# Recurrence heads of a two-layer transformer kernel: one head at a time through logarithms, or two at a time through products of gates

## The reference, cut to what matters

```python
def _hgrn2_direction(q, f_logit, v, lb):
    f = lb + (1.0 - lb) * sigmoid(f_logit)
    return _gla_chunkwise(q, 1.0 - f, v, log(f))
# S_t = diag(f_t) S_{t-1} + k_t v_t^T ;  o_t = S_t^T q_t     with k = 1 - f
o_fwd = _hgrn2_direction(q, ff, v, lb_fwd)
o_bwd = flip(_hgrn2_direction(flip(q), flip(fb), flip(v), lb_bwd))
o = rmsnorm(o_fwd + o_bwd, norm_g) * silu(hg)
```

## Time and profile before

| | |
|---|---|
| time, median of 3 runs | 2187.49 us (2187.25 to 2187.61) |
| profiled execution, span from first to last instruction | 2186.0 us |
| TensorE, matmuls | 2164.6 us busy, 99% |
| TensorE, weight loads | 1817.7 us, 83% |
| VectorE / ScalarE | 1452.0 us, 66% / 1031.1 us, 47% |
| HBM | 227 GB/s over the span |
| granted TensorE clock | 0.999 of full speed |

### The profile page before, as it was taken

The page is one execution under the profiler, slowest core; times in us unless marked ns, Lnnn a source line. Parts: engine busy times, 40 slices in busy tenths (PEclk is TensorE's granted clock), DMA queues, the critical chain, the costliest instruction groups (busy, mean ns, idle before and its releaser), DMA issues.

```text
span 2186.0 us, 25174 instructions
## 1 busy us (share of the span) xinstructions
PE 2164.6 (99%) x10675; PEld 1817.7 (83%) x10675; DVE 1452.0 (66%) x1415; ACT 1031.1 (47%) x1034; POOL 5.5 (0%) x17
## 2 busy tenths in 40 slices
PE   8999999999999999999999999999999999999998
PEld 8878888877888788778889988888888888888886
DVE  5778667775775777877866676484646645654756
ACT  5443573343435743443464556575434433443442
POOL 0000000000000000000000000000000000000000
PEclk9999999999999999999999999999999999999999
DMA  8867648584996548649853325374756656655753
GB/s 287 313 237 289 235 170 346 216 305 155 371 337 240 209 186 334 247 185 344 315 201 109 121 102 184 116 263 162 267 194 226 221 194 209 248 192 193 269 189 119
DMA packets 73071, 497.28 MB, mean 227 GB/s; under 512 B 9040, under 2 KB 9472, under 8 KB 16384
## 3 DMA queue, kind: packets, MB, share of 16 engines
q1 hardware_dynamic: 72640, 495.59, 62.2%
q10 hardware_dynamic: 320, 0.09, 0.0%
HBM read 491.42 MB, written 4.23 MB: 227 GB/s over the span
## 4 chain that ended last, share of the span: by engine, by line
PE 95%; DVE 3%; DMA 1%; ACT 1%; issue 0%; DVEq 0%; SPq 0%; ACTq 0%
PE products L2525 51%; PE products L2536 14%; PE aside L2525 6%; PE products L3260 4%; PE aside L3260 4%; PE products L3262 2%; PE aside L3262 2%; PE aside L2691 1%; PE aside L2845 1%; PE aside L2964 1%; DMA raw<-in_w_a_idx 1%; DMA raw<-in_w_mlp 1%; DVE w_low L1555 1%; PE products L2907 0%; PE aside L2659 0%; ACT w_high L885 0%
## 5 line engine op out<-in xcount | busy, mean ns | idle before, releaser
L1555 DVE TENSOR_TENSOR w_low<-raw,w_high 128x2048 fp32r<-128x2048 f32 (+3 forms) x319 | 704.3, 2211 | 501.0 <-ACT w_high L885 500.3
L885 ACT ACTIVATE w_high<-raw 128x2048 fp32r<-128x2048 f32 (+3 forms) x319 | 590.0, 1852 | 776.2 <-PE products L2525 412.4
L2525 PE MATMUL products<-w_high,x_high_and_low 128*128 128x512 f32 (+2 forms) x2496 | 756.0, 381 | 10.1 <-DVE w_low L1555 9.1
L2525 PEld LDWEIGHTS products<-w_high,x_high_and_low 128*128 128x128 f32 x2496 | 462.3, 189 | 97.0 <-issue 11.4
L2525 PE MATMUL products<-w_low,x_high_and_low 128*128 128x512 f32 (+2 forms) x1248 | 472.2, 378 | 0.0
L2525 PEld LDWEIGHTS products<-w_low,x_high_and_low 128*128 128x128 f32 x1248 | 235.5, 189 | 42.5 <-issue 1.7
L2536 PE MATMUL products<-w_high,x_high_and_low 128*128 128x512 f32 (+1 forms) x784 | 260.4, 393 | 0.0
L1569 DVE SCALAR_TENSOR_TENSOR raw<-raw,cond_row 128x2048 f32<-128x2048 f32 x96 | 219.2, 2284 | 0.0
L2536 PEld LDWEIGHTS products<-w_high,x_high_and_low 128*128 128x128 f32 x784 | 147.4, 188 | 25.9 <-issue 0.6
L2536 PE MATMUL products<-w_low,x_high_and_low 128*128 128x512 f32 (+1 forms) x392 | 150.4, 384 | 0.0
L2525 PE MATMUL products<-w_high,u_high 128*128 128x512 f32 x304 | 118.4, 390 | 0.0
(11 more groups left out here) (416 smaller groups left out, 2549.2 us busy)
## 6 DMA issues: line engine op xcount, KB each, us to landing
raw<-in_w_mlp SPq DMA_DIRECT2D x128, 1024.0 KB, 4.9
raw<-in_w_mod SPq DMA_DIRECT2D x96, 1024.0 KB, 5.1
raw<-in_w_ple SPq DMA_DIRECT2D x32, 1024.0 KB, 6.7
raw<-in_w_a_qkv SPq DMA_DIRECT2D x24, 1024.0 KB, 6.2
raw<-in_w_b_kvq SPq DMA_DIRECT2D x24, 1024.0 KB, 7.4
raw<-in_w_a_gate SPq DMA_DIRECT2D x16, 1024.0 KB, 6.1
raw<-in_w_a_out SPq DMA_DIRECT2D x16, 1024.0 KB, 7.1
raw<-in_w_b_gate SPq DMA_DIRECT2D x16, 1024.0 KB, 6.0
```

The lines of the kernel that those rows point to most:

```text
L885: act.activation(split_tile(m, 0, st, u, j, 0, n), m.raw[:, RAW_SLOT[at], 0:n], ACT.Copy).then_inc(m.s_w_high, 1)
L1555: dve.tensor_tensor(lo, m.raw[:, RAW_SLOT[at], 0:n], hi.bitcast(F32), ALU.subtract).then_inc(m.s_raw_used, 1)
L2525: ins = pe.matmul(bank, x[:, x0 + kk, a], w, start=first and kk == 0 and n == 0, stop=last and kk == st.kq - 1 and n == 2)
```

## The change

Two heads are now one batch, four batches of 12 steps, and a step is one of the 48 slots. Logarithms, the table of spans, its DMAs and its rounding, the span matmuls and the exponentials are gone. In their place the gates themselves are transposed (they were before too, but only to make k = 1 - f) and kept. VectorE keeps for both heads four strips of 512 (`m.h_w`: two kinds of keys, two kinds of queries) and doubles their spans level by level, starting with neighbours: the right halves of one pair of strips times the product of the left span's gates, the left halves of the other times the right span's, and then the spans' own products for the next level (`spans_doubled`). Before each doubling ScalarE lays out from these strips the level's keys and queries, two copies of 512 (`m.h_op`, two buffers in turn). TensorE multiplies them a step later, four matmuls into one of the two banks of `m.t`, and VectorE takes the level's pairs under its mask a step after that. TensorE may not write a bank of `m.t` for level i before VectorE has taken level i - 2 out of it (`s_h_red`). The last batch ends in slot 47; nothing of the heads is left in `uq`.

The core of the diff, ScalarE's part first, then VectorE's, then TensorE's:

```diff
+def crossed(x, left, right, half):
+
+
+    d = kind(x, left)
+    return bass.AP(tensor=d.tensor, offset=d.offset, ap=[d.ap[0], [2 * half, BH * T // (2 * half)], [BH * T * (right - left) + half, 2], [1, half]])
...
+def span_products(m, i):
+
+
+    return m.h_f[:] if i == 0 else m.h_p[:, 1024 - (2048 >> i):1024 - (1024 >> i)]
...
+        b, step = divmod(n, STEPS)
+        if step == 0:
...
+            forget = m.g[:, 2:4].rearrange("p h (d t) -> p d h t", d=2)
+            act.activation(m.h_qt[:], m.u[:, 0], ACT.Copy).then_inc(m.s_h_qc, 1)
+            act.activation(m.h_f[:].rearrange("p (d h t) -> p d h t", d=2, h=BH), forget, ACT.Copy).then_inc(m.s_h_fc, 1)
+            keys = m.h_w[:].rearrange("p (d h t) -> p d h t", d=4, h=BH)[:, 0:4:3]
+            act.activation(keys, forget, ACT.Identity, scale=-1.0, bias=1.0).then_inc(m.s_h_k1, 1)
+        if step == 3:
...
+        i = step - 2
+        if 0 <= i < LEVELS - 1:
+            half, k = 1 << i, (LEVELS - 1) * b + i
+            act.wait_ge(m.s_h_mul, LEVELS * b + i + 1)
+            if i == 0:
+                act.wait_ge(m.s_h_k1, b + 1)
+            if k >= 2:
+                act.wait_ge(m.s_h_am, products_before(k - 2) + 1)
+            for n, (left, right) in enumerate(((0, 3), (1, 2))):
+                operand = kind(m.h_op[:, k % 2], n).rearrange("p (s a e) -> p s a e", a=2, e=half)
+                act.activation(operand, crossed(m.h_w, left, right, half), ACT.Copy).then_inc(m.s_h_op, 1)
...
+    def chosen(b, i):
+
+
+        own = m.h_at[:, b % 2, 0].rearrange("p h b t -> p (h b) t")
+        mask = m.h_mask[:, LEVELS - 2 - i:LEVELS - 1 - i, :].broadcast_to((P, BH * RB, P))
+        dve.wait_ge(m.s_h_red, (LEVELS - 1) * b + i)
+        dve.copy_predicated(own, mask, m.t[:, i % 2].rearrange("p (a t) -> p a t", t=P)).then_inc(m.s_h_red, 1)
...
+    def spans_doubled(i):
+
+
+        half = 1 << i
+        totals = span_products(m, i).rearrange("p (s a) -> p s a", a=2)
+
+        def by(side):
+            return totals[:, :, side:side + 1].broadcast_to((P, totals.shape[1], half))
+
+        suffixes, prefixes = (m.h_w[:, 2 * BH * T * n:2 * BH * T * (n + 1)].rearrange("p (s a e) -> p s a e", a=2, e=half) for n in range(2))
+        lane.sync()
+        lane.did(dve.tensor_tensor(prefixes[:, :, 1, :], prefixes[:, :, 1, :], by(0), ALU.mult))
+        dve.tensor_tensor(suffixes[:, :, 0, :], suffixes[:, :, 0, :], by(1), ALU.mult).then_inc(m.s_h_mul, 1)
+        if i < LEVELS - 2:
+            lane.did(dve.tensor_tensor(span_products(m, i + 1), totals[:, :, 0], totals[:, :, 1], ALU.mult))
 
...
     def heads_slot(n):
...
-        if h < HH and s == 3:
-            dve.wait_ge(m.s_h_qc, h + 1)
-            decayed(h, 0)
-        if h < HH and s == 5:
-            decayed(h, 1)
-            if h + 1 < HH:
-                log_f_low(h + 1)
+        b, step = divmod(n, STEPS)
+        if step == 1:
+            dve.wait_ge(m.s_h_qc, b + 1)
+            dve.wait_ge(m.s_h_fc, b + 1)
+            back, forward = kind(m.h_w, 1), kind(m.h_w, 2)
+            lane.did(dve.tensor_tensor(forward, m.h_qt[:], m.h_f[:, 0:BH * T], ALU.mult))
+            dve.tensor_tensor(back, m.h_qt[:], m.h_f[:, BH * T:2 * BH * T], ALU.mult).then_inc(m.s_h_mul, 1)
+            dve.wait_ge(m.s_h_k1, b + 1)
+            dve.tensor_tensor(m.h_ks[:], kind(m.h_w, 0), kind(m.h_w, 3), ALU.add).then_inc(m.s_h_kc, 1)
+        i = step - 2
+        if 0 <= i < LEVELS - 1:
+            dve.wait_ge(m.s_h_op, 2 * (LEVELS - 1) * b + 2 * i + 2)
+            if i == 0:
+                dve.wait_ge(m.s_h_kc, b + 1)
+            spans_doubled(i)
+        i = step - 4
+        if 0 <= i < LEVELS - 1:
+            dve.wait_ge(m.s_h_am, LEVELS * b + i + 1)
+            if i == 0:
+                dve.wait_ge(m.s_h_a0, b + 1)
+            chosen(b, i)
...
-    def spans(h, group, dr, banks):
-
-        md = m.h_md[:, dr]
-        for blk in range(RB):
-            bank = banks[:, blk]
-            for first, lf in ((True, m.h_lfh[:, dr, blk]), (False, m.h_lfl[:, dr, blk])):
-                if group:
-                    ins = pe.matmul(bank, lf, md[:, 5:9, :].rearrange("p l t -> p (l t)"), start=first, stop=not first)
...
-        ins.then_inc(m.s_h_d, 1)
...
+        i = step - 3
+        if 0 <= i < LEVELS:
+            k = (LEVELS - 1) * b + i
+            if i < LEVELS - 1:
+                pe.wait_ge(m.s_h_op, 2 * k + 2)
+            else:
+                pe.wait_ge(m.s_h_mul, LEVELS * b + LEVELS)
...
+            if i >= 2:
+                pe.wait_ge(m.s_h_red, k - 1)
+            for hh in range(BH):
+                for blk in range(RB):
+                    own, other = T * hh + P * blk, T * hh + P * (1 - blk)
+                    if i < LEVELS - 1:
+                        keys, queries = m.h_op[:, k % 2, own:own + P], m.h_op[:, k % 2, BH * T + own:BH * T + own + P]
+                    else:
+                        keys, queries = kind(m.h_w, 3 * blk)[:, own:own + P], kind(m.h_w, 2 - blk)[:, other:other + P]
+                    ins = pe.matmul(m.t[:, i % 2, own:own + P], keys, queries, start=True, stop=True)
             ins.then_inc(m.s_h_am, 1)
...
-            if st is uq and j == 0:
-                heads_slot(6 * HH + 2)
...
             if st is uq and j == 2:
-                heads_slot(6 * HH + 5)
```

More of the change, by code:

```diff
@@ L43 @@
 LEVELS = 8
+BH, STEPS = 2, 12
+BATCHES = HH // BH
 WORDS = 24704
@@ L808, in unit_by_unit @@
                     bring(m.h_l0[:, dr, slot, :], rows(lb[slot], 1024), m.s_h_rows)
[L809 to L812, removed]
     for name in ("c_f", "c_hq", "c_hi", "c_mla", "c_hg", "uq", "ukv"):
@@ L1208, in scalar_program @@
     high_unit("c_hq", 0, [3])
-    def log_f(u):
-        act.wait_ge(m.s_h_fr, u + 1)
-        act.activation(m.h_lf[:, :, 512 * u:512 * u + 512], m.pf[:, :, 512 * u:512 * u + 512], ACT.Ln).then_inc(m.s_h_logf, 1)
[L1214 to L1218, removed]
-        else:
-            log_f(3)
-    gemm("c_hq", queries, late=2)
-    def log_f_high(h):
-        if h:
-            act.wait_ge(m.s_h_d, 4 * h)
-        else:
-            act.wait_ge(m.s_h_logf, 4)
-        lf = m.h_lf[:].rearrange("p r (a c) -> p a r c", a=2)[:, :, :, HD * h:HD * h + HD]
-        act.activation(m.h_lfh[:], lf, ACT.Copy).then_inc(m.s_h_lfh, 1)
@@ L2224, in vector_program @@
     ukv = PLAN["ukv"]
[L2225 to L2226 removed]
+    h_mean_squares(slice(0, HH - BH), HH - BH)
+    h_mean_squares(slice(HH - BH, HH), HH)
+    h_inverse_std(slice(0, HH - BH), 1)
     for rb in range(RB):
@@ L3301, in shape_constants @@
     rates = np.tile(np.concatenate([inverse(500000.0, ROT_A), inverse(500000.0, ROT_I), inverse(10000.0, ROT_M)]), (P, 1))
-    tau, spans = s, np.zeros((P, 2, 9, P))
-    def span(mid, right):
-        fwd = np.where(right, (mid <= tau) & (tau <= t), (t < tau) & (tau < mid))
-        bwd = np.where(right, (mid <= tau) & (tau < t), (t <= tau) & (tau < mid))
-        return fwd, bwd
-    def level(l):
-        half = P >> l
-        return span(t // (2 * half) * (2 * half) + half, t % (2 * half) >= half)
-    order = [span(P, np.zeros((1, P), bool))] + [level(l) for l in range(1, 4)]
-    order += [span(0, np.ones((1, P), bool))] + [level(l) for l in range(4, LEVELS)]
-    for n, pair in enumerate(order):
-        for dr in range(2):
-            spans[:, dr, n] = pair[dr]
     masks = [(s // (P >> l) // 2 == t // (P >> l) // 2) & (s // (P >> l) != t // (P >> l)) for l in range(1, LEVELS)]
     masks = np.ascontiguousarray(np.stack(masks, axis=1).reshape(P, -1), dtype=np.uint8)
-    out = {"consts": const, "rates": rates, "spans": spans.reshape(P, -1)}
+    out = {"consts": const, "rates": rates}
     return {"level_masks": masks, **{k: np.ascontiguousarray(v, dtype=np.float32) for k, v in out.items()}}
@@ L3398, in program @@
     d.rates = a["rates"]
-    d.spans = a["spans"]
     d.level_masks = a["level_masks"]
```

288 lines of the change are left out of this document (86 added, 202 removed).

## The result

The changed kernel takes 2160.65 us (median of 4 runs, 2160.51 to 2162.70) where the kernel before took 2187.51 beside it (2187.25 to 2187.61): 26.9 us less, a ratio of 0.988 (95% interval 0.9868 to 0.9892). The forecast was 2161.5, and its range 2155 to 2169. The profiled execution's span is 2158.7 us, 27.3 less than 2186.0. The 0.4 between the two gains comes from comparing executions: wherever both are on record, the time lies 1.9 to 2.0 us above the span in the changed kernel and 1.8 to 1.9 in the kernel before, so the span of 2186.0 belongs to an execution of some 2187.8, and the 1.5 given with it in front is too small.

The account below looks back on a forecast made before the run. TensorE's full list in the heads' stage was taken as the bound: 32.5 us shed less 6.5 of waits gives 26.0, so the median falls from 2187.5 to 2161.5 us; range 2155 to 2169.

Parts of the forecast that it names:

- What bounds the stage: Heads' stage: TensorE, busy 201.67 of 201.98 us, sets the time, so whatever leaves its list leaves the time.
- The spans' 31.0: TensorE in the heads: removing the span matmuls, 3.88 us for each of 8 heads, saves 31.0 us.
- The rest of the shed: TensorE beyond the spans: 1.5 us from dense operands, 0.9 from a vanished wait, less 0.9 for added returns.
- The strided operands: TensorE's level products: dense copies replace queries read in short runs, saving 0.19 us per head, 1.5 in all.
- the 0.9 priced for the added returns: TensorE: more returns from plain f32 to rounded weights, 44 instead of some 33 at 0.085 us, cost 0.9 us.
- The waits' 6.5: TensorE's level slots: nine waits for VectorE's choosing, 5.1 us, plus 1.4 of restarts, cost 6.5 us.
- the slot-by-slot walk: All 48 slots, each instruction starting when engine and semaphores allow: 5.1 us of waits, 2.2 in batch 3.
- ScalarE's copies: ScalarE's level copies: pace 0.51 us, level 0 perhaps 0.77 for single elements; no cost taken, up to 1.5 us allowed.
- No waits at all: Rival for the level slots: the chain has cover enough, only TensorE's list counts, 2155.0 us; chance 0.10.
- A chain that paces most slots: Rival for the level slots: dearer chain instructions give waits of 9 to 14 us, 2164 to 2169; chance 0.20.
- Rival 3: Level slots: chain at 1.8 times the price, waits pass 32.5 us, slower than before; 2197 at twice; chance 0.03.
- A return of the time in `uq`: Rival in `uq` or the MLA: ScalarE or VectorE holds TensorE later, 1 to 3 us; full return has chance 0.02.

Follow-up runs that it names:

- half the spans: The kernel before with the h_log_f_low matmuls left out of every call of spans, half of the span matmuls; 2173.69 us.
- the run with 1.2 us a level: The changed kernel with two more 512-wide VectorE products ahead of the doubling in six of a batch's seven levels; 2181.84 us.
- the choosing ahead: The changed kernel with VectorE's choosing of level i-2 placed ahead of the doubling for level i; 2154.11 us.
- both edits of the order: The changed kernel with VectorE's choosing ahead of its doubling and the rotation of the MLA's shared key moved from slot 40 to 46; 2153.53 us.
- dense copies: The changed kernel with ScalarE's copies of levels 0 and 1 reading one dense strip instead of elements in turn from two; 2160.62 us.

## Why the prediction was right, step by step

**What bounds the stage.** Held. The list of TensorE was the time before (half the spans: 15.6 off the list, 14.7 off the stage; 13.5 off the time), and it still is: 171.94 of 176.87 us.

**The spans' 31.0.** Held by the same run: half of them is 15.5 by my rows and 15.6 by its busy time.

**The rest of the shed.** The sum was 32.5. Measured it is 35.0: stage and `uq` are 28.0 shorter, in spite of slots 7.0 us longer than undisturbed ones. The term mis-sized is that of the plain f32 matmuls and their turns. The strided operands cost 2.0, not 1.5. And I priced a group of level products at 8 times 0.107 and 0.085 for the return, from a run of 16; the rows after:

```profile
1123.20 1.05 PE L2949 MATMUL aside<-h_operands 128*128 128x128 f32 x8
1124.01 0.48 PE L2493 MATMUL products<-w_high,x_high_and_low 128*128 128x512 f32 x1
1124.32 0.40 PE L2493 MATMUL products<-w_low,x_high_and_low 128*128 128x512 f32 x1
```

The group takes 0.81, not 0.86, which is 32 times 0.045 or 1.4 us. Its eight starts are 0.11 apart (1.05 less the last record's 0.27, over seven), and the rounded matmul behind it starts only some 0.03 after the last. So short groups are cheaper than a share of a long one, and this more than offsets the 0.9 priced for the added returns. The remaining 0.6 us of the 2.5 I don't split.

**The waits' 6.5.** Measured 7.0: 4.8 in seven brackets (5.1 in nine forecast; by batch 0.5, 1.2, 0.7 and 2.4 for 0.7, 1.1, 1.1 and 2.2) and 0.2 a wait around them where I took 0.15, with small delays in slots that show no bracket. The place and size of the largest, 2.10 in slot 42 for 2.2, came out of the slot-by-slot walk, and so did its cause: without the rotation it is 0.27. The mechanism (level i - 2 chosen one doubling too late) is shown three ways: by another order, by a third bank, and by longer work on VectorE.

**ScalarE's copies.** Level 0 has a pace of 0.75 where I expected "perhaps 0.77", level 1 0.61 where I expected 0.51. The prediction's nearest row was read a little too clean: the seventh of VectorE's eight products lasts 0.48, not 0.42, and the strips are 513 and 1537 elements apart, not 1024 or more. The Trainium skill (SBUF — State Buffer, section "Door 1: The DMA port swizzle") puts the limit at two accesses in a 16-byte line, by which runs of two would be free; on ScalarE they paid 0.10 a copy, and only runs of four were free. I held the whole at 0 to 1.5 us; it is at most 0.5.

**The rivals.** No waits at all (2155.0) failed, and is what one bank more makes true. A chain that paces most slots failed: seven of 28 level slots wait. The run with one product more shows how near it was: 0.6 us on VectorE a level, and the gain falls from 26.9 to 17.1. Rival 3's price was 0.48 on six instructions a pair of slots, some 1.4 us a level, from where it would pass 2187; the run with 1.2 us a level stands at 2181.84, so the point was about right. A return of the time in `uq` failed (27.25 us, 2.9 less, as forecast); but 1.0 us does come back later, 0.7 of it at the wait for `mix` (the offset between the two traces is 28.1 us ahead of that wait and 27.4 behind it).

**Why the median was met.** 35.0 less 7.0, and 0.2 for the earlier start, less 1.0 that came back, is 27.2, the span's 27.3. I had 26.0 by a shed 2.5 too small, waits 0.5 too small, and nothing for `mix`: the errors cancel in part.

**What stays open.** The wait for `mix` is 0.5 us here, 0.5 with half the spans, 0.3 with three banks, none with the choosing ahead, and 0.5 again with both edits of the order. In each kernel with a shorter heads' stage ScalarE has a wait of 1.0 to 1.8 us there for a transfer of `in_w_mlp`, 0.8 and 0.4 in the two with the long one. The kernel with one product more has that wait (1.0) and none for `mix`. Why the transfer comes later relative to the work wasn't tried, and neither was whether it causes TensorE's wait. Open too is what the lower clock costs in a stage that has other waits (above).

## What to carry to other kernels

When a chain over two engines feeds a full TensorE, walk its slots with measured prices and ask at each PSUM bank who must read it before the next write; what stands between that read and its data in the reader's queue is the wait. Issue the read that frees a bank ahead of work that waits for something else, or give the bank a third partner: 6 to 7 us here, for no work more. Average idle time (VectorE's third) says nothing of this. And a walk is only as good as the place of each instruction in its queue: two products on the wrong side of a wait made a forecast of 6.6 us where 10.6 came.

## What the runs showed of the hardware

- TensorE's granted clock fell to 0.50 behind waits of 2.26, 2.32, 2.60, 2.71 and 3.25 us, for 3 to 7 us; the slot around it took 1.6 to 2.6 us longer. Only behind 3.25 us did it fall within the wait. In the other five cases, that of 2.04 us (below) among them, it was still 1.00 when TensorE started again, and fell 0.4 to 1.4 us later, with TensorE busy. It stayed at 1.00 behind 2.10 us in the changed kernel (and 2.12 with dense copies), but fell behind 2.04 us with one product more, in `c_mla`. So the length of the wait alone doesn't decide. The wait of slot 42 may cost twice in some executions: one of the changed kernel's four took 2162.70 us at a mean granted clock of 0.998, the others 2160.51 to 2160.67 at 0.999; with dense copies two took 2161.03 and 2161.53 at 0.998, two 2160.08 and 2160.22 at 0.999; and the 16 of the four kernels without that long wait all show 0.999 and agree within 0.7 us in each kernel. No trace of a 0.998 execution of these two kernels was taken.
- A moving operand in runs of 8 elements and fewer, in turn from two strips, cost plain f32 matmuls of 128 columns 0.03 us each (0.25 for 8 matmuls, 16 records, with the turn behind them).
- ScalarE's 512-wide copy, from one to the next: 0.75 us for single elements in turn from two strips, 0.61 for runs of two, 0.51 for four and more. VectorE's doubling with a step of two in one strip (0.69) shows no surcharge.
